# Alternating the order of the high and the low matmul from chunk to chunk

## The reference

```python
# first block
h = rmsnorm(x, g_mix)
z = h @ w_in                                  # 2048 -> 10248: convolution, attention and gate inputs
merged = gc * (conv_y @ w_conv_out) + ga * (attn @ w_attn_out)
x = x + merged @ w_mix_out
u = square(relu(rmsnorm(x, g_mlp) @ w_ff1))   # 2048 -> 8192
x = x + u @ w_ff2                             # 8192 -> 2048
x = rmsnorm(x, g_final)
# second block, with shifts, scales and gates from c
mod = silu(c) @ w_ada + b_ada
h = rms_norm(x, norm_mix_g) * (1 + scale_m) + shift_m
proj = h @ w_in_2                             # attention and state-space inputs
x = x + gate_m * (concat([attn, ssm]) @ w_out)
h = rms_norm(x, norm_ffn_g) * (1 + scale_f) + shift_f
u = causal_dwconv_2(h @ w_up, conv_w, conv_b) # 2048 -> 11264
g, val = split(u, 2)
x = x + gate_f * ((silu(g) * val) @ w_down)   # 5632 -> 2048
return rms_norm(x, final_norm_g)
```

## Time and profile before

| | |
|---|---|
| median of 3 runs | 2641.5 us (2636.43 to 2641.7) |
| profiled execution, its own time | 2632.75 us |
| its span | 2631.0 us |
| mean granted clock of TensorE | 0.987 |
| busy: TensorE, its weight loads, VectorE, ScalarE | 2547.4, 2205.4, 2036.8, 1329.1 us |
| matmuls | 14384 |
| read from HBM | 559.12 MB |

### The profile page before, as it was taken

The page is one execution under the profiler, slowest core; times in us unless marked ns, Lnnn a source line. Parts: engine busy times, 40 slices in busy tenths (PEclk is TensorE's granted clock), DMA queues, the critical chain, the costliest instruction groups (busy, mean ns, idle before and its releaser), DMA issues.

```text
span 2631.0 us, 47703 instructions
## 1 busy us (share of the span) xinstructions
PE 2547.4 (97%) x14384; PEld 2205.4 (84%) x14384; DVE 2036.8 (77%) x3152; ACT 1329.1 (51%) x2047; POOL 5.2 (0%) x13
## 2 busy tenths in 40 slices
PE   7999999999999999999998999979899999999998
PEld 6888888888888888888886888868688888888886
DVE  7778675579887887877888457686788888888888
ACT  5344434565554543544554347544445545546456
POOL 0000000000000000000000000000000000000000
PEclk9999999999999999999998999999899999999999
DMA  8776673557888888888885554315455655556554
GB/s 291 270 268 206 225 266 128 173 186 250 277 276 283 275 288 279 279 284 275 283 279 173 179 185 148 136 54 186 140 185 166 203 190 167 203 179 186 195 172 154
DMA packets 160540, 561.90 MB, mean 214 GB/s; under 512 B 17987, under 2 KB 18284, under 8 KB 160492
## 3 DMA queue, kind: packets, MB, share of 16 engines
q1 hardware_dynamic: 132284, 459.04, 51.8%
q10 hardware_dynamic: 27792, 101.20, 11.5%
q0 software_dynamic: 416, 1.06, 0.2%
HBM read 559.12 MB, written 2.11 MB: 213 GB/s over the span
## 4 chain that ended last, share of the span: by engine, by line
PE 93%; DVE 4%; issue 1%; ACT 1%; DMA 1%; DVEq 0%; SPq 0%; ACTq 0%
PE bank L284 93%; DVE w_lo L919 1%; DVE scratch L1247 1%; DVE R L952 0%; DMA X<-in_x 0%; DVE ss L982 0%; ACT w_hi L545 0%; DMA ada_w<-in_w_ada 0%; PE bank L398 0%; PE bank L389 0%; DVE ss L1353 0%; DVE Z L1501 0%; DVE G L1390 0%; DVE scratch L952 0%; ACT H L574 0%
## 5 line engine op out<-in xcount | busy, mean ns | idle before, releaser
L284 PE MATMUL bank<-H,w_hi 128*128 128x512 f32 x4672 | 1654.1, 398 | 30.8 <-DVE H L1253 16.1
L284 PE MATMUL bank<-H,w_lo 128*128 128x256 f32 x4672 | 1314.3, 281 | 0.0
L919 DVE TENSOR_TENSOR w_lo<-w_raw,w_hi 128x1024 fp32r<-128x1024 f32 x900 | 1092.2, 1222 | 142.3 <-ACT w_hi L545 134.4
L284 PEld LDWEIGHTS bank<-H,w_hi 128*128 128x128 f32 x4672 | 881.8, 189 | 242.4 <-issue 26.2
L545 ACT ACTIVATE w_hi<-w_raw 128x1024 fp32r<-128x1024 f32 x900 | 911.0, 1051 | 1.0 <-DMA w_raw<-in_w_up 0.7
L284 PEld LDWEIGHTS bank<-H,w_lo 128*128 128x128 f32 x4672 | 888.6, 190 | 0.1
L284 PE MATMUL bank<-U,w_hi 128*128 128x512 f32 x1984 | 702.0, 397 | 5.4 <-DVE U L1482 4.8
L284 PE MATMUL bank<-U,w_lo 128*128 128x256 f32 x1984 | 558.4, 281 | 0.0
L560 ACT ACTIVATE scratch<-bank 128x256 f32<-128x256 f32 x356 | 136.7, 384 | 823.2 <-PE bank L284 823.2
L284 PEld LDWEIGHTS bank<-U,w_hi 128*128 128x128 f32 x1984 | 372.4, 188 | 98.9 <-DVE U L1482 6.1
L284 PEld LDWEIGHTS bank<-U,w_lo 128*128 128x128 f32 x1984 | 374.0, 189 | 0.0
(11 more groups left out here) (197 smaller groups left out, 1166.6 us busy)
## 6 DMA issues: line engine op xcount, KB each, us to landing
w_raw<-in_w_ff SPq DMA_DIRECT2D x256, 512.0 KB, 5.2
ada_w<-in_w_ada ACTq DMA_DIRECT2D x192, 512.0 KB, 4.6
w_raw<-in_w_up SPq DMA_DIRECT2D x176, 512.0 KB, 4.0
w_raw<-in_w_z SPq DMA_DIRECT2D x96, 512.0 KB, 4.7
w_raw<-in_w_in SPq DMA_DIRECT2D x88, 512.0 KB, 3.9
w_raw<-in_w_gate SPq DMA_DIRECT2D x64, 512.0 KB, 4.9
w_raw<-in_w_down SPq DMA_DIRECT2D x64, 384.0 KB, 3.0
w_raw<-in_w_down SPq DMA_DIRECT2D x64, 320.0 KB, 3.3
```

Of the source, the lines that this page charges most:

```text
L284: return nc.tensor.matmul(out, lhsT, rhs, start=start, stop=stop, skip_group_check=True)
L919: TT(w_lo[:, slot, :], w_raw[:, slot, :], w_hi[:, slot, :].bitcast(F32), ALU.subtract)\
```

## The change

In unit, an even chunk of a piece keeps its order (high, then low), and an odd chunk gets the other one (low, then high). The signal at the end of the piece goes with whichever matmul is last: the high one in pieces of 8 and 6, the low one in pieces of 5. The start flag stays with the high matmul of chunk 0, the stop flag with the low matmul of the last chunk.

```diff
                     dst = bank[2 * h + par] if two_banks else bank[par]
+                    def high(c):
+                        start = c == 0 and (h == 0 or two_banks)
+                        return mm(dst[:, :], w_hi[:, 2 * par + h, c * P:(c + 1) * P], buf[:, k0 + c, :], start, False)
+
+                    def low(c):
+                        stop = c == n - 1 and (h == 1 or two_banks)
+                        return mm(dst[:, T:2 * T], w_lo[:, 2 * par + h, c * P:(c + 1) * P], buf[:, k0 + c, 0:T], False, stop)
+
                     for c in range(n):
                         if par == 0 and operand and c % 2 == 0:
 
                             pe.wait_ge(sem(operand), operand_base + k0 + min(c + 2, n))
-                        lhs = slice(c * P, (c + 1) * P)
-                        start = c == 0 and (h == 0 or two_banks)
-                        stop = c == n - 1 and (h == 1 or two_banks)
-                        mm(dst[:, :], w_hi[:, 2 * par + h, lhs], buf[:, k0 + c, :], start, False)
-                        end = mm(dst[:, T:2 * T], w_lo[:, 2 * par + h, lhs], buf[:, k0 + c, 0:T], False, stop)
+                        if c % 2 == 0:
+                            high(c)
+                            end = low(c)
+                        else:
+                            low(c)
+                            end = high(c)
                     end.then_inc(sem("piece_used"), 1)
```

## The result

The changed kernel has a median of 2622.17 us over 4 runs (2621.72 to 2624.17), the kernel before one of 2638.97 over 4 (2635.19 to 2641.7). The ratio is 0.9948, 95% interval 0.9933 to 0.9963: faster by half a per cent, and outside of the 0.2% within which the likeliest case had put it, inside of the range. The profiled execution took 2622.47 us, with a span of 2620.7 and a mean granted clock of 0.989.

The account below looks back on a forecast made before the run. The prediction took TensorE's streamed matmuls on line 284 to bound the kernel. High to high gave -3 us and all other terms zero, so 2641.5 - 3 = 2638 us, with a range of 2612 to 2662.

Parts of the forecast that it names:

- the likeliest case: Whole kernel: mix of quick and slow stretches about as now, 2638 us, within 0.2% of no change; chance 0.38.
- TensorE's pace is the bound: Matmuls of line 284: TensorE is busy 97% of the span, in long unbroken runs of matmuls.
- Loads hidden one ahead, so order costs nothing: Weight loads on TensorE: each matmul hides exactly one load, before and after, so reordering costs zero.
- low to low: A low matmul started after a low one: taken as 0.118 us, between 0.11 and 0.12, cost zero.
- High to high from the narrow product, 0.2319: A high matmul after a high one: 0.2319 us from sixteen matmuls against narrow weights, -3 us over 3,424 steps.
- The mix of paces stays about as now: Matmul stretches: 37% quick at 0.3467 us a chunk, the others slow at 0.3534, as before the change.
- all quick: Rival: the new row puts every stretch on the quick pace, -29 us, 2612; chance 0.34, shared with a shorter low to low.
- all slow: Rival: no stretch settles into the quick pace, +17 us, 2658; chance 0.26, shared with longer high-to-high steps.
- 2641.5 as the start of the sum: Whole kernel: the -3 us from a profiled execution of 2632.75 us carries over to the median of 2641.5, giving 2638.
- the exposed load: Rival: the second low matmul's load isn't hidden and low to low takes 190 ns, +247 us, 2888; chance 0.02.
- one pace everywhere that isn't in the mix now: Sign of being wrong: all matmul stretches at a single pace other than 0.3467 or 0.3534 us a chunk.
- Loads and read bandwidth: TensorE's load port: loads take no read bandwidth from the running matmul, so a new order of loads changes zero.

Follow-up runs that it names:

- x4_by_piece: Changed kernel, but with all high matmuls of a piece first and then all its low ones: 2633.32 us, 0.9988 of the kernel before.
- x5_short_loads: Kernel before, order kept, with weight loads of 32 columns in place of 128 except at a bank's first chunk, leaving out three quarters of the products: 2584.93 us.
- y3_aligned_after: Changed kernel with 32 bytes of padding ahead of X, so that H and the weights move together: 2614.55 us, 0.991 of the kernel before.
- y4_aligned_before: Kernel before, in its alternating order, with 32 bytes of padding ahead of X: 2645.5 us, 1.0035 of the kernel before.

## Why the prediction was right or wrong, point by point

- **TensorE's pace is the bound.** Right. VectorE's, ScalarE's and the loads' counts and durations didn't change, and the whole gain is in distances between matmuls. VectorE is busy 51.35 of 60 us in the same window of ff1 (880 to 940) where the earlier trace rows had 52.07.
- **Loads hidden one ahead, so order costs nothing.** The hidden load held: low to low takes 0.1147 on H and 0.1178 on U, inside of the 0.11 to 0.12 that bounded it, and no load is exposed. The conclusion was wrong, since it took the streaming of a matmul to be a constant. x4_by_piece shows it isn't: the same step low to low on H takes 0.1189 in another row.
- **High to high from the narrow product, 0.2319.** It measured 0.2329 on both operands, a miss of 1 ns the other way (+3 us by itself); low to low on H was over-sized by 3 ns (0.118 taken, 0.1147 measured). But pricing single steps was the failed step: on H the remaining steps low to high fell as well (from 0.1167 to 0.1159).
- **The mix of paces stays about as now.** This is the assumption that failed, and with it the likeliest case (2638; measured 2622.17). The prediction had seen that the pace is a state which the same code falls into, and gave the two rivals "all quick" and "all slow". There was a third: a pace of its own for the new row, 0.3484 and 0.3514, which is met in every stretch.
- **2641.5 as the start of the sum.** The profiled execution was 8.75 us below the median, and the text let the difference carry over. But the sum was made with 37% quick chunks, which was this execution's draw. The repeated profile had fewer (H at 0.3518 against 0.3495). Against this one's draw the new paces are worth 10 us by the spans; against that of the medians 17, or some 14 by the larger sets of runs.
- **Rivals.** All slow and the exposed load didn't come. All quick was right in sign and in its reason (a changed rhythm frees the slow stretches), and too large: 29 us, against 16.8 by the medians and some 14 by the ratio. The range was wide enough to hold both rivals, so that the time fell inside of it says nothing for the likeliest case.
- **What it said would show it.** The windows (341 to 349), the two-chunk steps (0.697 and 0.703, between 0.693 and 0.707) and the run of 4,032 matmuls (705.61, between 700 and 712) all held, and yet the likeliest case fell: these marks were too wide to tell it from a gain. Of its signs of being wrong one came true, "one pace everywhere that isn't in the mix now".
- **Loads and read bandwidth.** The Trainium skill (TensorE: Matmul & The Clock Gate, "Step-by-step: what each phase is for") says that a load takes no read bandwidth from the running matmul. The runs don't settle that: with loads of 32 columns in place of 128 a chunk of U took 0.3411 in place of 0.3533 (x5_short_loads), which speaks against it, but fewer output rows were written too, and nothing separates the two.

## What to carry to other kernels

When matmuls follow each other without a gap, read the distance from start to start over some tens of them, by stage and by operand, and in two executions. Where it takes two values for one code, the median hides a draw: price a change against the mix over several profiles, and don't carry a difference from one of them over. If such distances exceed the streaming of the columns, the order of sizes and the byte distance between moving operand and weights are worth a run each; here they gave 0.5% and 0.3% more, and the worth of one hung on the other (the gap of y3_aligned_after gained with the order in twos, that of y4_aligned_before lost 0.35% with the alternating one).

## What the runs showed of the hardware that was not expected

- fp32r matmuls of 512 and 256 columns with a load each take 0.3467 to 0.3533 us together at full clock, where 768 columns at 2.4 GHz are 0.320; at 1.2 GHz they take 0.64, nothing above the columns.
- The excess is set by a periodic row of steps, with cycles of one to four chunks (ten for U in the changed kernel). It goes with the order of sizes, with the places in bytes of operand and weights, and in the alternating order with chance: one program, two profiles, up's second group with the group of down ahead of it in 180.98 and in 183.29 us.
- 32 bytes of padding changed a pace by up to 0.0047 us a chunk (U in twos: 0.3514 to 0.3467), 1.3%.
